# Eight of twelve branch-gate weight units computed as seven quarter products behind the mLSTM, their gates kept in DRAM, and the later modulation under the attention

## The reference, cut to what matters

```python
mod = silu(cond) @ w_ada + b_ada                 # six vectors of 1024, for two conditions
h   = rmsnorm(x) * (1 + scale1) + shift1
(na_q, na_k, na_v, m_q, m_k, m_v, m_o, m_i, m_f, cv_b, cv_c, cv_x, gate_pre) = split(h @ w_in)
g   = sigmoid(gate_pre + b_gate)                 # three branches x 1024 channels
merged = g0*(att @ w_br_na) + g1*(hm @ w_br_m) + g2*(hc @ w_br_cv)
x   = x + gate1 * rmsnorm(merged @ w_out)
h2  = rmsnorm(x) * (1 + scale2) + shift2
x   = x + gate2 * rmsnorm((silu(h2 @ w_g) * (h2 @ w_u)) @ w_down)
```

## Time and profile before

| | us |
|---|---|
| median of 3 runs (1138.38 to 1138.59) | 1138.51 |
| the profiled execution, its own time | 1139.12 |
| its span in the profile | 1137.2 |
| PE busy / DVE busy / ACT busy / POOL busy | 1119.5 / 724.0 / 477.5 / 70.5 |
| weight blocks loaded by SP (512 KB each) | 182 in `raw` |

### The profile page before, as it was taken

One profiled execution on the slowest core, in us unless ns is written; L12 is line 12 of the kernel. 1 busy time (PEld: TensorE's weight loads), 2 busy tenths in 40 slices (PEclk: granted clock), 3 DMA queues, 4 the chain that ended last, 5 costly groups with the idle time before them and its releaser, 6 DMA issues.

```text
span 1137.2 us, 18483 instructions
## 1 busy us (share of the span) xinstructions
PE 1119.5 (98%) x7324; PEld 1058.7 (93%) x7324; DVE 724.0 (64%) x1297; ACT 477.5 (42%) x881; POOL 70.5 (6%) x123
## 2 busy tenths in 40 slices
PE   6999999999999999999999999999999999999997
PEld 4799999899999999999999988999999999988886
DVE  5734545458575655687885446899897777633444
ACT  5534444344333343322222338655555555533431
POOL 2051101000000000400000002000000000000002
PEclk9999999999999999999999999999999999999999
DMA  9675221132621112345653235143332242325112
GB/s 366 235 218 128 72 76 43 34 111 80 75 70 56 56 58 96 108 130 186 201 186 115 83 121 169 55 167 130 114 110 75 75 148 76 113 66 192 56 37 93
DMA packets 40150, 130.22 MB, mean 115 GB/s; under 512 B 8736, under 2 KB 10304, under 8 KB 38528
## 3 DMA queue, kind: packets, MB, share of 16 engines
q1 hardware_dynamic: 36592, 121.41, 33.1%
q0 software_dynamic: 3472, 7.62, 2.4%
HBM read 121.64 MB, written 7.36 MB: 113 GB/s over the span
## 4 chain that ended last, share of the span: by engine, by line
PE 92%; DVE 4%; ACT 1%; issue 1%; DMA 1%; SPq 0%; POOL 0%; POOLq 0%; ACTq 0%; DVEq 0%
PE ps L2120 28%; PE ps L2122 28%; PE ps L2121 28%; PE ps L2367 1%; PE ps L2382 1%; PE ps L2341 1%; PE ps L2429 1%; PE ps L2431 1%; PE ps L2433 1%; DMA xt<-in_x_sample 1%; PE ps L2308 0%; PE ps L2167 0%; PE ps L2417 0%; DVE w_lo L1502 0%; PE ps L2415 0%
## 5 line engine op out<-in xcount | busy, mean ns | idle before, releaser
L2122 PE MATMUL ps<-h_hi,w_lo 128*128 128x320 f32 x1184 | 365.9, 309 | 0.0
L2120 PE MATMUL ps<-h_hi,w_hi 128*128 128x320 f32 x1024 | 321.3, 314 | 0.2 <-DVE w_hi L1627 0.2
L2121 PE MATMUL ps<-h_lo,w_hi 128*128 128x320 f32 x1024 | 316.4, 309 | 0.0
L2122 PEld LDWEIGHTS ps<-h_hi,w_lo 128*128 128x128 f32 x1184 | 222.2, 188 | 0.0
L1502 DVE TENSOR_TENSOR w_lo<-raw,w_hi 128x1024 fp32r<-128x1024 f32 x109 | 132.7, 1227 | 111.7 <-ACT w_hi L1122 111.0
L2120 PEld LDWEIGHTS ps<-h_hi,w_hi 128*128 128x128 f32 x1024 | 192.4, 188 | 1.9 <-issue 1.2
L2121 PEld LDWEIGHTS ps<-h_lo,w_hi 128*128 128x128 f32 x1024 | 192.4, 188 | 0.1
L2120 PE MATMUL ps<-w_hi,h_hi 128*128 128x512 f32 x378 | 148.7, 393 | 0.0
L2122 PE MATMUL ps<-w_hi,h_lo 128*128 128x512 f32 x378 | 147.2, 389 | 0.0
L2121 PE MATMUL ps<-w_lo,h_hi 128*128 128x512 f32 x378 | 147.2, 389 | 0.0
L1122 ACT ACTIVATE w_hi<-raw 128x1024 fp32r<-128x1024 f32 x109 | 113.3, 1052 | 32.2 <-PE ps L2122 31.4
(11 more groups left out here) (284 smaller groups left out, 1823.3 us busy)
## 6 DMA issues: line engine op xcount, KB each, us to landing
raw<-in_w_blocks SPq DMA_DIRECT2D x182, 512.0 KB, 3.8
ada<-in_w_first SPq DMA_DIRECT2D x8, 1024.0 KB, 20.2
xline<-x SPq DMA_DIRECT2D x5, 512.0 KB, 5.1
x<-xline SPq DMA_DIRECT2D x5, 512.0 KB, 7.6
xt<-in_x_sample SPq DMA_DIRECT2D x4, 512.0 KB, 6.5
condr<-in_cond_rows POOLq DMA_DIRECT2D x2, 1024.0 KB, 7.8
vtok<-vline POOLq DMA_DIRECT2D x8, 256.0 KB, 9.4
g<-gline SPq DMA_DIRECT2D x2, 1024.0 KB, 6.7
```

Source lines behind the costliest of these rows:

```text
L2120: nc.tensor.matmul(dst, wh, xh, start=first, stop=False, skip_group_check=resumed)
L2121: nc.tensor.matmul(dst, wh, xl, start=False, stop=False, skip_group_check=resumed)
L2122: return nc.tensor.matmul(dst, wl, xh, start=False, stop=last, skip_group_check=resumed)
```

## The change

- The gate units of branches 0 and 1 (eight units) leave their places before their branch units and are computed together, right behind the two `mo` units, as wide units 0 to 7 (`NG = 8`); the FFN's wide units become 8 to 27. Before them the four quarters of h are put together again by POOL (`h_hi + h_lo`, step `reb`), summed by DVE (`gsum`) and split (`gsplit`) during the `mo` groups.
- Each unit's gates (tanh) go to `stage`, are stored to a DRAM tensor `gdram` and fetched per branch unit into `gt` or `gt2` (`gload`). The eight branch units then follow one another.
- The head norm's steps stand inside wide units: `hm 0` and `hm 1` of chunk c behind product 2 of units 2c and 2c+1, `hm 2` behind product 4 of the odd one; chunk 4 stands around the first group of the first branch unit.
- The 24 `ada` blocks move from the gate units to the q, k, mq, mk and mv units, under the attention, with silu(cond) in `condr_a`; the second product of each pair is written over the block itself.
- The attention's values are fetched per pair of units (four gathers of 128 rows of 512 bytes) instead of eight gathers of 2 KB rows at once.
- Splitting the attention's result (`att_split`) stands in the last gate unit, the split of hm (`hm_split`) in the second branch unit.

```diff
-ADA_AHEAD, ADA_PER_GATE = 2, {2: (0, 0, 0, 0), 0: (1, 4, 4, 4), 1: (4, 4, 1, 0)}
+NG = 8
+def adas_behind(kind, which, p):
+    if kind == "mv":
+        return 4 if p == 3 else 0
+    if (kind, which) == ("mk", 1):
+        return 2 if p == 0 else 0
+    if kind in ("q", "k", "mq", "mk") and (kind, which) != ("q", 0):
+        return 1 + p
+    return 0
+        behind = {0: [("ada_turn", 2), ("ada_store", 2)],
+                  1: [("wsum", 0), ("wop", 0, 0), ("wop", 0, 1)],
+                  2: [("gsum", 0)],
+                  3: [("gsum", 1), ("gsum", 2), ("gsplit", 0), ("wop", 0, 2), ("wop", 0, 3)],
+                  4: [("gsplit", 1), ("gsum", 3)],
+                  5: [("gsplit", 2), ("wop", 0, 4), ("wop", 0, 5)],
+                  7: [("gsplit", 3)]}
+        plan.append(("reb",))
+        for j in range(8):
+            ...
+            group("mo", UNIT_OF[("mo", m)], f, h)
+            plan.extend(behind.get(j, []))
+        for w in range(NG):
+            c = w // 2
+            for q in range(7):
+                plan.append(("wu", w, q))
+                if q == 2:
+                    plan.append(("hm", w % 2, c))
+                if q == 4 and w % 2:
+                    plan.append(("hm", 2, c))
+                ...
+                if w == NG - 1:
+                    if q in (1, 3, 5, 6):
+                        split_to(d0 + (1, 3, 5, 6).index(q) + 1)
+                    if q in (3, 5):
+                        plan.append(("att_split", q // 2 - 1))
+        plan.append(("gates_end",))
+        plan.append(("gload", 1))
+        for u in range(8):
+            n = UNIT_OF[("br", divmod(u, 4))]
+            b = BLOCK_OF[n, 0]
+            for j, emit in enumerate(tiles(n)):
+                if j == 0:
+                    plan.append(("use", b))
+                if j == (0 if u < 7 else 2):
+                    split_to(b + BLOCKS_HELD)
+                if u == 0 and j < 2:
+                    plan.extend([("hm", 0, 4)] if j == 0 else [("hm", 1, 4), ("hm", 2, 4)])
+                if (u, j) == (1, 0):
+                    plan.append(("hm_split",))
+                ...
+                if j == 1 and 1 <= u < 7:
+                    plan.append(("gload", u + 1))
+                emit()
 # ScalarE, split of a weight block
+                elif B0 <= b < B0 + BLOCKS_HELD:
+                    act.wait_ge(fp_done, 7 * (NG - 1) + (2, 4, 6, 7)[b - B0])
+            def gate_unit(w, q):                       # ScalarE
+                ...
+                elif q == 2:
+                    snapshot(w, 1)
+                    gate_tanhs(w, 0)
+                elif q == 3:
+                    ...
+                    snapshot(w, 2)
+                elif q == 4:
+                    ...
+                    snapshot(w, 3)
+                elif q == 5:
+                    ...
+                    gate_tanhs(w, 1)
+                    ...
+                else:
+                    gate_tanhs(w, 2)
 # VectorE, first ada block
-                    dve.wait_ge(condr_rd, 1)
+                    dve.wait_ge(condr_rd, 2)
 # ScalarE, use of k unit 0
+                    if UNITS[n][:2] == ("k", 0) and part == 0:
+                        act.wait_ge(condr_in, 32)
+                        nc.scalar.activation(condr_a[:, :, :], condr_a[:, :, :], ACT.Silu).then_inc(condr_rd, 1)
 # GpSimd, h put together again
+                    pool.wait_ge(ml_h, len(ML_UNITS))
+                    pool.wait_ge(merged_add, 16)
+                    for dst, k0, h in ((tq12, 0, 1), (tq22, 4, 1), (tq11, 0, 0), (tq21, 4, 0)):
+                        nc.gpsimd.tensor_tensor(dst[:, :, :], h_hi[:, k0:k0 + 4, half(h)].bitcast(F32),
+                                                h_lo[:, k0:k0 + 4, half(h)].bitcast(F32),
+                                                ALU.add).then_inc(reb_done, 1)
 # TensorE, first product of a wide unit
+                if w == 0 and q == 0:
+                    pe.wait_ge(act_drain, drains("A", gid("mo", 1, 1, 1)))
```

More of the change, by code:

```diff
@@ L83, in weight_units @@
         u += [("cc", p, KD, UW), ("cx", p, KD, UW), ("cb", p, KD, UW)]
[L84 to L91, removed]
+    for i in range(4):
+        u += [("gate", (2, i), KD, UW), ("br", (2, i), 4, UW)]
+    u += [("mo", 0, KD, UW), ("mo", 1, KD, UW)]
+    u += [("br", (b, i), 4, UW) for b in range(2) for i in range(4)]
     for c in range(2):
@@ L97, in weight_units @@
             u.append(("down", (c, i), DOWN_TILES[i], 512))
+    u += [("ada", (m, j), KD, P) for m in (2, 4, 3) for j in range(KD)]
     return u
@@ L104 @@
 WU = FK - 2
+WT = NG + WU
 QUARTER = (0, 1, None, None, None, None, 3)
@@ L117, in parts_of, with block_order @@
     return 0 if kind == "mif" else kc * w // 1024
-BLOCKS = [(n, p) for n in range(len(UNITS)) for p in range(parts_of(n))]
+def adas_behind(kind, which, p):
[6 more added lines that the diff above has]
+    return 0
+def block_order():
+    late = [n for n in range(FIRST_ADA, len(UNITS)) if UNITS[n][0] == "ada"]
+    order = []
+    for n in range(len(UNITS)):
+        if UNITS[n][0] != "ada":
+            for p in range(parts_of(n)):
+                order.append((n, p))
+                order += [(late.pop(0), 0) for _ in range(adas_behind(*UNITS[n][:2], p))]
+    assert not late
+    return order
+BLOCKS = block_order()
 BLOCK_OF = {np_: b for b, np_ in enumerate(BLOCKS)}
@@ L216, in unit @@
             later = 0
[L217 to L233, removed]
+            if j % 2 == 0 and j // 2 < parts_of(n):
                 plan.append(("use", BLOCK_OF[n, j // 2]))
@@ L350, in make_plan @@
                         if t == TT - 1:
-                            split_to(BLOCK_OF[n, j] + BLOCKS_HELD + 1)
-            else:
+                            split_to(BLOCK_OF[n, j] + 2 * BLOCKS_HELD + 1)
+            elif kind == "mo" and which == 0:
+                assert not side
+                gate_stretch()
+            elif kind != "mo" and (kind != "br" or which[0] == 2):
                 unit(n)
[L354 to L357, removed]
         if kind == "k":
@@ L367, in make_plan @@
                 side += [[("ml", 0, s)], [("ml", 1, s)]]
[L368 to L374, removed]
         n += 1
@@ L560, in place @@
                            cb=C_CB)[kind] + which * UW + part * P
-WU_PLACES = [place("fg" if w % 2 == 0 else "fu", 1 + w // 2, f) for w in range(WU) for f in range(2)]
+WU_PLACES = [place("gate", divmod(w, 4), f) for w in range(NG) for f in range(2)] + [place("fg" if w % 2 == 0 else "fu", 1 + w // 2, f) for w in range(WU) for f in range(2)]
 ADA5_PLACES = [place("ada", (5, j), 0) for j in range(KD)]
@@ L1453, in _ @@
                     operand_hi(step[1], step[2])
+                elif step[0] == "wu" and step[1] < NG:
+                    gate_unit(step[1], step[2])
                 elif step[0] == "wu":
@@ L1709, in wide_unit @@
                         operand_lo(1, 0)
+                elif q in (2, 3, 4):
+                    if more:
+                        operand_lo(w + 1, q - 1)
+                elif q == 5:
+                    if more:
+                        operand_lo(w + 1, 4)
+                    gate_collect(w, 1)
+                else:
+                    gate_collect(w, 2)
+                    if more:
+                        operand_lo(w + 1, 5)
+            def wide_unit(w, q):
+                more = w + 1 < WT
+                if q == 0:
+                    if w % 2 == 0 and w > NG:
+                        collect(w - 1, 3)
+                    operand_lo(w, 6)
+                    if more and w > NG:
+                        weight_sums(w + 1)
+                elif q == 1:
+                    if more and w > NG:
+                        operand_lo(w + 1, 0)
+                    collect(w, 0)
+                    if w == NG:
+                        weight_sums(w + 1)
+                        operand_lo(w + 1, 0)
                 elif q == 2:
@@ L2160, in group @@
                     bank_free(g)
+                if kind == "br" and which == (0, 0):
+                    pe.wait_ge(gate_tanh, 4 * (NG - 1))
+                    pe.wait_ge(fz, NG - 1)
+                    pe.wait_ge(fy, NG - 1)
+                    pe.wait_ge(hm_out, 3)
                 if kind == "ada_row":
```

464 lines of the change are left out of this document (305 added, 159 removed).

## The result

The changed kernel takes 1146.35 us (median of 4 runs, 1145.62 to 1147.14), the kernel before 1138.55 us beside it. The ratio is 1.0068, 95% interval 1.0051 to 1.0086: slower by 7.8 us, where the forecast was +1.0 and the range ended at 1145. The span of the profiled execution is 1144.6 us, 7.4 more than before.

The account below looks back on a forecast made before the run. TensorE's instruction count was taken to set the end, other engines costing only where PE waits. -14.1 + 0.8 + 9.8 + 2.0 + 2.5 = +1.0 us: 1140.1 profiled, 1139.5 for the median; range 1131 to 1145.

Parts of the forecast that it names:

- Matmuls removed: Gate stretch: eight gate units take 12.32 us instead of 14.08, with no stall inside; 14.1 us gained.
- Entry: Start of the gate stretch: first product waits for the last `mo` drain, rebuild hidden; 0.8 us lost, bounds 0.5 and 3.5.
- Exit: From last gate product into branch groups: PE waits for queued splits and chunk 4's norm; 9.8 us lost, bounds 4.8 and 12.
- Clock: Behind the exit's 7 us gap: branch groups run at half pace for a while; 2.0 us lost, bounds 0 and 4.
- Attention: Modulation blocks on DVE under the attention delay PE in two places; 2.5 us lost together, bounds 0 and 8.
- the stall at k unit 0: Under the attention: first modulation block delays the lo split of k unit 0's second slice; 0.5 us lost.
- the gates by DRAM: Branch units: gate fetches go out a unit ahead and four free banks cover the rest; no cost, otherwise 7 us.
- No wait at all: Faster rival: the change pays its matmuls, only the entry's 0.8 us is lost; 1125.2 us, chance 0.07.
- POOL's rebuild is late: Slower rival at the entry: the rebuild of h costs +2.7 us; 1142.2 us, chance 0.06 shared with late DRAM gates.
- the gates' way through DRAM: Slower rival in the branch units: gate fetches come late, +7 us; 1146.5 us, chance 0.06 shared with the late rebuild.
- a VectorE that falls behind under the attention: Slower rival: some five pairs each hand 1.1 us of lag to PE, attention costs 8 us; 1145.0 us, chance 0.14.
- three signs of being wrong: PE's longest exit wait under 4 us, clock at 1.00 behind a 7 us gap, or PE waiting at most attention pairs.

Follow-up runs that it names:

- e10_exit_clear: e6_all plus an own, earlier-fetched buffer for branch unit 1's gates, last two branch blocks' splits ahead of the last tanhs, `hm_split` behind branch unit 2: 1128.40 us, ratio 0.9909.
- e1_rebuild_on_vector: The changed kernel with the four adds that rebuild h moved from GpSimd to VectorE, behind `mo` groups 0, 0, 1 and 2: 1139.69 us, ratio 1.0011.
- e2_splits_after_drains: The changed kernel with the first split of the sums behind `mo` group 6, the other three behind group 7; rebuild stays on GpSimd: 1142.68 us, ratio 1.0037.
- e6_all: The changed kernel with the rebuild on VectorE, chunk 4 inside the gate stretch and the second half of the `at` split one product earlier: 1131.93 us, ratio 0.9940.
- e13_best: e10_exit_clear with ScalarE's SiLU at q unit 0's second block and the first product waiting only for its own bank's `mo` group: 1128.09 us, ratio 0.9903.
- e3_chunk4_inside: The changed kernel with mLSTM chunk 4's normalization moved from the first branch unit into the gate stretch, all five chunks over eight units: 1139.91 us, ratio 1.0013.

## Why the prediction failed

*Matmuls removed, -14.1: right.* Units of 12.32 us with no stall inside, and e10_exit_clear brings the whole gain to the end of the kernel.

*Entry, +0.8: this step failed.* It measured 8.1. It was put as "the rebuilt quarters are hidden", with an upper bound of 3.5 in case "POOL is half slower beside DVE". GpSimd was not slower than assumed: four adds took 13.6 us, 15.5 were assumed. The wait stands where the prediction had put it, at the first product for ScalarE's last `mo` drain, but it is 5.5 us and not 0.8. Three things were missed. VectorE's weight sums beside the adds take as long as the adds, 3.4 us each, so the harm the bound had asked about, to GpSimd, is small beside the one to VectorE. The drains of `mo` stand behind the splits in ScalarE's queue; the exit was worked out queue by queue, the entry was not, and `gsplit 2` ahead of the last drains is plain in the plan. And a gap of 5.5 us lowers the clock here as it does at the exit, 2.6 us more, which was priced only there. e1_rebuild_on_vector shows the adds on GpSimd as the source, e2_splits_after_drains the second as the way in which it reached PE.

*Exit, +9.8: right.* PE went on 11.76 us after the last product, where the working said 11.6; even the gap ahead of the second half of `at` is there (2.6, "2 to 3"). The one idle gap is 5.9, not 7. *Clock, +2.0: right*, 1.7 by the starts of the matmuls behind the gap. *Attention, +2.5:* about right in sum (2.6 to 3.5 by the stretch itself), in its places only in part; that the start of `mo` shows 2.3 is scatter. Pair 2 was named (1.6 instead of 2.0), the stall at k unit 0 didn't occur, and pairs 0 and 1 lost 0.8 and 1.0.

*At nothing: the gates by DRAM.* Right for this kernel and fragile: with the exit repaired, the fetch for unit 1 costs 1.9 us and 1.6 at the lower clock (e6_all) until it has a buffer of its own and goes out earlier.

*The rivals.* "No wait at all", 1125.2 with 0.07, is nearly what e13_best reaches (1128.1) after eight edits, so the plan's orders and one buffer were what the change lacked, not its idea. "POOL's rebuild is late" had the right place at a third of its size, but for a slower GpSimd, not for a VectorE that is held up. Two rivals come near the measured 1146.35 only by luck: the gates' way through DRAM (1146.5) cost this kernel nothing, and a VectorE that falls behind under the attention (1145.0) was priced at 8 us, of which the trace shows 2.6 to 3.5. None of the prediction's three signs of being wrong came: they were all about the exit, the clock and the attention, none about the entry.

## What to carry to other kernels

When work moves to an idle GpSimd, ask what VectorE does meanwhile: here, operations with two SBUF operands on both engines added most of their time instead of hiding it. Write out every in-order queue at each seam of a new stretch, the entry as carefully as the exit; a drain behind an operation that waits turns any lateness into a stall of TensorE. And price the lower clock for every gap, short ones too: here it added 2.6 us to the 5.5 of the entry, 1.7 to the 10 of the exit, 1.5 to a gap of 2.6 (e3_chunk4_inside) and 1.6 to one of 1.9 (e6_all).

## What the runs showed of the hardware

A GpSimd add of two 128x1280 fp32 operands takes 2.96 us alone and up to 3.94 beside a VectorE operation with two SBUF operands (the same add takes VectorE 1.48 to 1.73, e1_rebuild_on_vector); that operation then takes 3.34 to 3.9 us, whether its own length is 0.69 or 1.2. How a VectorE operation with one operand fares beside such an add, no run shows. Beside GpSimd's one-operand `mo` operations VectorE's 128x512 sums take 0.82 to 0.94 instead of 0.69. After the entry's gap of 5.5 us the granted clock was 0.54 on the mean of the next 6.1 us, after the exit's 5.9 us gap 0.66 over the next 5.3. It also fell behind shorter gaps: 0.50 over the 2.6 us behind one of 2.6 (e3_chunk4_inside), 0.65 over the 4.9 us behind one of 1.9 (e6_all). It stayed at 1.00 behind one of 2.1 at the entry (e2_splits_after_drains).
